# Gate tiles first: the order of projection tiles in a delta-rule stage on one Trainium2 core

## The reference, cut to what matters

```python
proj = einsum('bld,dp->blp', n, w_in)            # 1024 inputs
c = silu(centred_dwconv(conv_in, conv_w, conv_b))  # 7 taps over tokens
q, k, v = ...                                    # per head 128 wide
q = l2_normalize(q) * 128 ** -0.5
k = l2_normalize(k)
o_fw = gated_delta_chunked(q, k, v, g_fw, sigmoid(b_f))
o_bw = flip_seq(gated_delta_chunked(flip_seq(q), ...))
o_gdn = rms_norm(o_fw + o_bw, gdn_norm_w) * silu(g_gate)
```

## Time and profile before

| | us |
|---|---|
| median of three runs | 4174.6 |
| the profiled execution's own time | 4184.94 |
| its span in the trace | 4182.9 |
| of it the stage `gdn` | about 82 to 715 |

### The profile page before, as it was taken

One profiled execution on the slowest core, in us unless ns is written; L12 is line 12 of the kernel. 1 busy time (PEld: TensorE's weight loads), 2 busy tenths in 40 slices (PEclk: granted clock), 3 DMA queues, 4 the chain that ended last, 5 costly groups with the idle time before them and its releaser, 6 DMA issues. The chain is left out here.

```text
span 4182.9 us, 39643 instructions
## 1 busy us (share of the span) xinstructions
PE 3490.6 (83%) x15252; PEld 2489.6 (60%) x15252; DVE 1768.7 (42%) x2609; ACT 1053.6 (25%) x1591; POOL 269.5 (6%) x222
## 2 busy tenths in 40 slices
PE   4988885888867786999768779998999777869997
PEld 3465565344643234888645457887888655447886
DVE  2748755456340003442324645433442333644433
ACT  2121121022210003221211633223221311633222
POOL 1110010011020001000011000000000111000001
PEclk7999997889879998999876989999999876979998
DMA  2101000010207952221201013222222201002221
GB/s 79 51 21 41 21 1 20 31 51 0 81 12 305 420 239 72 98 93 71 97 19 41 1 41 114 97 101 81 92 100 80 81 25 51 1 41 101 92 99 60
DMA packets 49393, 326.26 MB, mean 78 GB/s; under 512 B 6896, under 2 KB 7280, under 8 KB 11120
## 3 DMA queue, kind: packets, MB, share of 16 engines
q1 hardware_dynamic: 49264, 324.52, 20.7%
HBM read 321.35 MB, written 2.10 MB: 77 GB/s over the span
## 5 line engine op out<-in xcount | busy, mean ns | idle before, releaser
L358 PE MATMUL psum<-ffn_x_hi,ffn_w_hi 128*128 128x512 f32 x1408 | 551.7, 392 | 14.1 <-DVE ffn_x_lo L314 14.1
L358 PE MATMUL psum<-ffn_x_lo,ffn_w_hi 128*128 128x512 f32 x1408 | 550.7, 391 | 0.0
L358 PE MATMUL psum<-ffn_x_hi,ffn_w_lo 128*128 128x512 f32 x1408 | 550.5, 391 | 0.0
L303 DVE TENSOR_TENSOR ffn_w_lo<-ffn_raw,ffn_w_hi 128x2048 fp32r<-128x2048 f32 x128 | 293.4, 2292 | 420.7 <-ACT ffn_w_hi L274 420.7
L104 PE MATMUL psum<-mix_normed,mix_ring 128*128 128x512 f32 x832 | 375.8, 614 | 67.2 <-DMA mix_ring<-w_ssd 32.6
L274 ACT ACTIVATE ffn_w_hi<-ffn_raw 128x2048 fp32r<-128x2048 f32 x128 | 245.2, 1916 | 572.9 <-PE psum L358 572.8
L104 PEld LDWEIGHTS psum<-mix_normed,mix_ring 128*128 128x128 f32 x832 | 163.4, 198 | 277.0 <-issue 233.5
L358 PEld LDWEIGHTS psum<-ffn_x_hi,ffn_w_hi 128*128 128x128 f32 x1408 | 266.4, 189 | 75.3 <-DVE ffn_w_lo L310 20.2
L358 PEld LDWEIGHTS psum<-ffn_x_lo,ffn_w_hi 128*128 128x128 f32 x1408 | 266.4, 189 | 55.6
L358 PEld LDWEIGHTS psum<-ffn_x_hi,ffn_w_lo 128*128 128x128 f32 x1408 | 266.1, 189 | 55.8
L358 PE MATMUL psum<-ffn_hid_hi,ffn_w_hi 128*128 (+1 forms) x704 | 273.9, 389 | 0.0
(11 more groups left out here) (413 smaller groups left out, 5452.9 us busy)
## 6 DMA issues: line engine op xcount, KB each, us to landing
ffn_raw<-w_ffn SPq DMA_DIRECT2D x128, 1024.0 KB, 4.8
mix_ring<-w_experts SPq DMA_DIRECT2D x48, 1024.0 KB, 13.7
mix_ring<-w_mix SPq DMA_DIRECT2D x38, 1024.0 KB, 4.8
mix_normed<-w_experts SPq DMA_DIRECT2D x24, 1024.0 KB, 14.7
experts_work<-w_experts SPq DMA_DIRECT2D x24, 1024.0 KB, 15.7
mix_ring<-w_gdn SPq DMA_DIRECT2D x16, 1024.0 KB, 4.8
mix_ring<-w_ssd SPq DMA_DIRECT2D x10, 1024.0 KB, 7.1
mix_ring<-w_out SPq DMA_DIRECT2D x8, 1024.0 KB, 6.6
```

The costliest lines, as they stand in the source:

```text
L303: dve.tensor_tensor(w_lo[:, q, :], raw[:, q, :], w_hi[:, q, :].bitcast(F32), ALU.subtract)\
L358: ins = pe.matmul(out, wp[:, q, w], xp, start=start and a == 0, stop=stop and a == 2)
```

## The change

For pairs 1 to 3 the eight tiles are computed in the order gates, q, k, v. A tile has now a **place** (0 to 7) that sets its slab and its bank: gates in places 0 and 1 (banks 0, 1), q in 2 and 3 (banks 2, 3), k in 4 and 5 (banks 0, 1), v in 6 and 7 (banks 2, 3). Places 4 and 5 wait for silu of the gates, places 6 and 7 for the convolution of q. ScalarE does silu of the gates at the beginning of a pair. Pair 0 keeps its order.

```diff
--- before.py
+++ after.py
@@ -720,6 +720,8 @@
     scal = lambda name, p, d, hh: m.scal[name][:, :, d, 2 * p + hh]
     by_chunk = lambda bank: m.ps[:, bank, :].rearrange("p (t i) -> p t i", t=NT)
     chunk = lambda s, d: s if d == 0 else NT - 1 - s
+    places = lambda p: (6, 7, 0, 1, 2, 3, 4, 5) if p else range(8)
+    place_of = lambda p, n: list(places(p)).index(n)
 
     with stage(nc, m, "gdn") as (block, sem):
         landed = sem(2)
@@ -738,7 +740,8 @@
                 for s in range(4 * p, 4 * p + 4):
                     if s >= 2:
                         sp.wait_ge(projected, 2 * s - 2)
-                    sp.dma_start(slab(s).rearrange("p k n -> p (k n)"), io["w_gdn"][s]).then_inc(landed[s % 2], 16)
+                    sp.dma_start(slab(s).rearrange("p k n -> p (k n)"),
+                                 io["w_gdn"][4 * p + places(p)[2 * (s % 4)] // 2]).then_inc(landed[s % 2], 16)
 
         @block.gpsimd
         def _(pool):
@@ -760,14 +763,18 @@
 
         @block.tensor
         def _(pe):
-            def tile(p, n):
-                s = 4 * p + n // 2
+            def tile(p, at):
+                s = 4 * p + at // 2
                 pe.wait_ge(landed[s % 2], 16 * (s // 2 + 1))
-                if n >= 4:
-                    pe.wait_ge(steps, 42 * p + 14 * (n // 2 - 1))
+                if p and at < 4:
+                    pe.wait_ge(nt_done, 4 * p)
+                elif p and at < 6:
+                    pe.wait_ge(silued, 8 * p + at - 3)
                 elif p:
-                    pe.wait_ge(nt_done, 4 * p)
-                product(pe, m.ps[:, n % 4, :], lambda k: slab(s)[:, k, n % 2 * P:n % 2 * P + P],
+                    pe.wait_ge(steps, 42 * p + 14)
+                elif at >= 4:
+                    pe.wait_ge(steps, 14 * (at // 2 - 1))
+                product(pe, m.ps[:, at % 4, :], lambda k: slab(s)[:, k, at % 2 * P:at % 2 * P + P],
                         lambda k: m.xT[:, k, :]).then_inc(projected, 1)
 
             def lengths(p):
@@ -923,27 +930,35 @@
                     act.wait_ge(added, 2 * q + hh + 1)
                     act.activation(back[hh], both[hh], ACT.Square).then_inc(o_squared, 1)
 
+            def gates(p):
+                for n in range(2):
+                    at = place_of(p, 6 + n)
+                    act.wait_ge(projected, 8 * p + at + 1)
+                    act.activation(m.mixed[:, 2 * p + n, :], m.ps[:, at % 4, :], ACT.Silu).then_inc(silued, 1)
+
             def project(p):
+                if p:
+                    gates(p)
+                early = 2 if p else 0
                 for n in range(6):
                     act.wait_ge(steps, 42 * p + 14 * (n // 2 + 1))
                     act.activation(c[:, n, :], c[:, n, :], ACT.Silu).then_inc(silued, 1)
                     if n == 1:
-                        act.wait_ge(silued, 8 * p + 2)
+                        act.wait_ge(silued, 8 * p + early + 2)
                         if p >= 2:
                             act.wait_ge(o_summed, 2 * (p - 1))
                         for hh in range(2):
                             act.activation(q_sq[:, p % 2, hh, :], c[:, hh, :], ACT.Square, scale=EPS ** 0.5 * P)\
                                 .then_inc(q_squared, 1)
                     if n == 3:
-                        act.wait_ge(silued, 8 * p + 4)
+                        act.wait_ge(silued, 8 * p + early + 4)
                         if p:
                             act.wait_ge(decays, 8 * p)
                         for hh in range(2):
                             act.activation(flat(k_sq[:, hh, :, :]), c[:, 2 + hh, :], ACT.Square)\
                                 .then_inc(squared, 1)
-                for n in range(2):
-                    act.wait_ge(projected, 8 * p + 7 + n)
-                    act.activation(m.mixed[:, 2 * p + n, :], m.ps[:, 2 + n, :], ACT.Silu).then_inc(silued, 1)
+                if p == 0:
+                    gates(p)
                 act.wait_ge(shifted, p + 1)
                 act.activation(k_rows, k_rows, ACT.Sqrt).then_inc(rooted, 1)
 
@@ -1022,8 +1037,9 @@
                     if p:
                         dve.wait_ge(qd_done, 4 * p)
                         dve.wait_ge(kb_done, 4 * p)
-                convolve(dve, m, [m.ps[:, n % 4, :] for n in two], [c[:, n, :] for n in two],
-                         [m.cols[:, 8 * n:8 * n + 8] for n in two], projected, [8 * p + n + 1 for n in two],
+                convolve(dve, m, [m.ps[:, place_of(p, n) % 4, :] for n in two], [c[:, n, :] for n in two],
+                         [m.cols[:, 8 * n:8 * n + 8] for n in two], projected,
+                         [8 * p + place_of(p, n) + 1 for n in two],
                          steps, 42 * p + 7 * a)
 
             def keys(p):
```

## The result

The changed kernel has a median of 4190.9 us over seven runs (4182.1 to 4197.3) against 4176.6 us for the kernel before over seven (4168.6 to 4183.3): ratio 1.0032, 95% interval 1.0017 to 1.0047. It is slower by 14.4 us in the medians. A second set, twelve runs against 23 of the kernel before, gave 1.0021 (1.0011 to 1.0031), 10.2 us. The forecast was 13.3 us. The profiled execution has a span of 4192.1 us, 9.2 more than the one of before, and the stages behind `gdn` keep their lengths.

The account below looks back on a forecast made before the run. The prediction took TensorE's gate tiles to bound the stretch's end and VectorE the convolution of q. Late q and the new tail, +12.1 us, plus clock, +1.2, on 4174.6 gave 4187.9 us; range 4180 to 4196.

Parts of the forecast that it names:

- The bound at each end: Convolution of q bound by VectorE, TensorE's tiles 5 us early; end bound by TensorE's gate tiles, VectorE about 9 us spare.
- The late q: Convolution of q waits for the third and fourth tile: 8.15, 11.60 and 13.01 us late in pairs 1 to 3.
- Pair 1: Inverse follows silu of v by 0.25 us and starts at 240.78 instead of 241.05: -0.3 us.
- Pairs 2 and 3: Inverse waits for the output shift behind keys and the root behind silu of v: +5.3 and +7.1 us.
- root to inverse: Pairs 2 and 3, from ScalarE's root to the inverse: 3.38 us, taken from the trace before the change.
- The clock: TensorE's clock at the first matmuls of the inverse, after 6 to 11 us idle: +0.3, +0.4 and +0.5 us.
- The sum: Whole kernel: 12.1 us for the three pairs plus 1.2 for the clock, +13.3 us, +0.32%.
- A: Rival: the lane inversion hides the gate tiles, q keeps its start; together -20.6 us, 4154 us; chance 0.04.
- B: Rival: the root isn't on the path in pairs 2 and 3, inverse follows silu of v; 4179 us; chance 0.10.
- second way: Grouped with B: full clock in all three inverses gives +7.3 us, 4182 us; within B's chance of 0.10.
- C: Rival: POOL slows the convolution of v, 3.4 us a pair, 10.2 more, 4198 us; chance 0.08.

Follow-up runs that it names:

- the experiment with the output matmuls: Changed kernel with the output matmuls of pairs 2 and 3 behind the fourth tile instead of the first; stretches 69.14, 72.59 and 72.71 us; one run, 4175.9 us.
- b_pool_later: Kernel before with POOL's decay tables of pairs 1 to 3 put off until the key tables are made; stretches 69.55, 70.77, 70.96 us; one run, 4179.8 us.
- a_shift_first: Changed kernel with the shift of the output ahead of the keys; stretches 69.12, 75.76 and 72.75 us; one run, 4177.7 us.
- tail_alone: Kernel before with gate tiles still last but in banks 5 and 4, their silu ahead of v's, lengths in bank 5; median 4162.0 us, ratio 0.9955.

## Why the prediction was right

**The bound at each end** was read rightly. The wait for the lengths went, and VectorE's chain from the late q took its place, as forecast; the experiment with the output matmuls shows the coupling, 3.43 us of q for 3.47 of stretch.

**The late q**, pair by pair: forecast 8.15, 11.60 and 13.01 us. Against the earlier trace rows, measured from the first tile, it was 8.15 in pair 1 (206.88 - 170.53 against 199.70 - 171.50), 11.57 in pair 2 and 11.58 in pair 3 (515.14 - 475.37 against 499.04 - 470.85). Pair 3 was over by 1.4: the forecast carried over the first tile of 8.49 us in the earlier trace rows, and in this execution it took 7.10.

**Pair 1**: forecast -0.3, measured -0.4. **Pairs 2 and 3**: forecast +5.3 and +7.1, measured +4.2 and +4.5. The term that was mis-sized in both is root to inverse, taken over as 3.38 us from the earlier trace rows; it measured 2.28 (392.87 to 395.15). The three key tables ran beside POOL before. In the changed kernel the lengths are summed earlier, POOL is through by 390.75, and they take 0.26 us instead of 1.36 (`b_pool_later` shows the same with nothing else moved). That is 1.1 us in each of the two pairs; the other 1.4 of pair 3 are its first tile. I had asked what POOL would slow at its new place, and not what it had been slowing at its old one.

**The clock** at the head of the inverse: forecast +1.2, measured +1.9 by what lies between the inverse and the next anchor. The 32 matmuls took 5.89, 6.62 and 5.36 us. Those of pair 2 are above the 5.73 of the earlier trace rows that I called nearest. One row was not enough for it, and the bounds held.

**The sum**: +13.3 forecast, +10.1 by the parts of the trace, of which 1.0 was given back ahead of pair 1, and 14.4 and 10.2 in the medians of two sets. The sign is right, and the size within the range. That the first median, 14.4, lies nearer to the forecast than the parts of the trace do is luck: part by part the forecast was 3.2 us high. The interval of the first set, 7 to 20 us, holds the 9.2 of the two traces.

A first tile at half clock may be in some of the unprofiled runs. Before, a slow first tile was covered by the lane inversion: in pair 3 of the earlier trace rows it took 8.49 us, and the convolution of q still ended 28.19 us after its start, as in the other pairs. With q as third and fourth tile and VectorE the bound to the end it is paid in full: 3.0 us in `a_shift_first`, pair 2. How often it happens in unprofiled runs was not measured.

**The rivals.** A, that the lane inversion hides the gate tiles, fell: 27.7 us of tiles don't fit in 19. Its price for the tail was nearly right nevertheless (20.6 against 18.0 in `tail_alone`, with one tile at half clock). B fell: the root was on the path, and moving the shift ahead of it gave 3.3 us in pair 3. Its second way, full clock in all three inverses, fell too: 5.89, 6.62 and 5.36 us against 3.74. C fell. POOL of the changed kernel, pair 2:

```profile
386.68 4.07 POOL L751 TENSOR_TENSOR mix_ring<-const_sb,mix_scalars 128x512 f32<-128x512 f32 x4 [89.93 <-PE psum L787]
```

It lies in the middle of the convolution of v (382.42), whose 12 L624 take 7.95 us as those of k do, 7.96, with no POOL beside them; in pairs 1 and 3 those of v take 7.96 beside POOL. By the Trainium skill (SBUF — State Buffer, "SBUF: two separate sides") a VectorE operation with two SBUF inputs contends with a GpSimd operation that reads SBUF. The key tables, which multiply two SBUF inputs, do (1.36 against 0.26), and a convolution step, with PSUM, one SBUF tile and an SBUF column, does not. Here the traces agree, if the column of this operation does not count as an input.

## What to carry to other kernels

Moving filler work to the front of a stage is free only where the engine behind has slack for all of it: compare the length of the filler (13.9 us) with the slack at that end (5 us in pair 1, under 2 in the others), not with the wait that goes at the other. When the filler is stuck at the tail only for want of a buffer, give it another buffer before giving it another place; here two PSUM banks that were already free were worth 18 us in the stretches, and putting a step that needs no root ahead of those that do took 4.8 us more off pair 2. And a duration taken from a row holds for the neighbours of that row: if the change moves what runs beside it, ask for both.

## What the runs showed of the hardware that I had not expected

Three multiplications of 16 columns took 1.36 us beside a POOL operation and 0.26 alone, five times as long. The longest single one took 1.02 us, about the length of one of POOL's four operations (4.09 us together), against a median of 0.17 in `b_pool_later`. That fits a wait for one whole POOL operation, but no run shows the wait itself.

The first tile of a pair took 6.9 us at full clock, and 8.5 or 10.1 in three of the 30 starts that the ten traces hold (granted clock 0.50 at the start). The 32 matmuls ahead of it start 6.69 us before it each time. In 23 starts these matmuls took 5.2 to 5.5 us, the pause behind them was 1.2 to 1.5, and the tile was at full clock. In the other seven they took 3.84, at full clock, and the pause was 2.85: then the tile was at full clock four times, all in pair 1, and slow three times, in pairs 2 and 3. So the low clock fell in one or the other, never in both. In the matmuls it cost nothing, since the tile starts 6.69 us behind their start either way; in the tile it is paid where TensorE's tiles are on the path. What decides between the two, no run shows.
